# Output matmuls dealt over the last head, query rotations ahead of a normalisation, modulation sums in two halves: a two-block fp32 network on one Trainium2 core

## What is computed

```python
# first block (layers one and two): attention of the second branch, and the merge of three branches
q = rms_norm(q, qn_g); k = rms_norm(k, kn_g)
q, k = rope_2d(q, tabs), rope_2d(k, tabs)
s = jnp.einsum('bqkgd,bskd->bkgqs', q, k) * (ATT_HD ** -0.5)
p = jax.nn.softmax(s, axis=-1)
...
xs = xs + gate_x * ((sigmoid(p[13]) * ya + sigmoid(p[14]) * yb + sigmoid(p[15]) * yc) @ w_out)

# second block (layers three and four): four mLSTM heads, four retention heads, one output product
ada = c_act @ w_ada[l] + b_ada[l]
shift, scale, gate = jnp.split(ada, 3, axis=-1)
...
y = jnp.concatenate([y_m, y_r], axis=-1) @ w_out[l]       # (512, 2048) @ (2048, 1024)
x = x + gate * y
```

## Time and profile before

| what | us |
|---|---|
| median of three runs | 3299.59 (3297.2 to 3299.6) |
| the profiled execution, its own time | 3300.26 |
| its span | 3298.3 |
| PE busy | 3164.9 (96%) |
| DVE busy | 1366.0 (41%) |
| POOL busy | 1539.9 (47%) |
| ACT busy | 846.0 (26%) |
| mean granted TensorE clock | 0.978 |

### The profile page before, as it was taken

The page is one execution under the profiler, slowest core; times in us unless marked ns, Lnnn a source line. Parts: engine busy times, 40 slices in busy tenths (PEclk is TensorE's granted clock), DMA queues, the critical chain, the costliest instruction groups (busy, mean ns, idle before and its releaser), DMA issues.

```text
span 3298.3 us, 40515 instructions
## 1 busy us (share of the span) xinstructions
PE 3164.9 (96%) x15123; PEld 2302.9 (70%) x15123; DVE 1366.0 (41%) x2573; ACT 846.0 (26%) x1547; POOL 1539.9 (47%) x1451
## 2 busy tenths in 40 slices
PE   7999998999999999998989999999998999999989
PEld 4666675665656555465778768888994688889955
DVE  3021346544564412226666555444332363443322
ACT  4122226421111022324411222332111123322111
POOL 1688987000000059971353325776550157775600
PEclk9999999999999999998999999999999999999999
DMA  6111110023443121110233422222221222222202
GB/s 222 52 39 32 31 35 14 14 79 125 128 138 130 41 64 39 45 39 1 68 115 116 140 66 77 72 70 77 65 77 51 66 77 77 65 77 65 76 28 75
DMA packets 259907, 236.59 MB, mean 72 GB/s; under 512 B 20950, under 2 KB 257410, under 8 KB 259716
## 3 DMA queue, kind: packets, MB, share of 16 engines
q1 hardware_dynamic: 259716, 234.02, 23.4%
HBM read 231.91 MB, written 2.10 MB: 71 GB/s over the span
## 4 chain that ended last, share of the span: by engine, by line
PE 86%; DVE 8%; POOL 2%; ACT 2%; issue 1%; SPq 1%; DMA 0%; DVEq 0%; ACTq 0%; POOLq 0%
PE ps L481 27%; PE ps L1219 23%; PE ps L526 11%; PE ps L1053 5%; PE ps L512 3%; DVE arena L1905 2%; PE ps L1277 2%; PE ps L796 2%; DVE arena L1909 1%; PE ps L1321 1%; PE ps L809 1%; ACT arena L1375 1%; PE ps L1158 1%; DVE bQz L1909 1%; DVE small L2176 1%
## 5 line engine op out<-in xcount | busy, mean ns | idle before, releaser
L2604 POOL TENSOR_TENSOR arena<-arena,posi 128x512 f32<-128x512 f32 (+1 forms) x360 | 412.3, 1145 | 30.0
L481 PE MATMUL ps<-hT,wring 128*128 128x512 f32 (+1 forms) x1184 | 406.4, 503 | 0.7 <-ACT arena L1375 0.7
L526 PE MATMUL ps<-hT,wring 128*128 128x512 f32 (+1 forms) x1024 | 376.9, 523 | 0.4 <-ACT arena L1375 0.2
L481 PEld LDWEIGHTS ps<-hT,wring 128*128 128x128 f32 x1184 | 228.3, 194 | 170.1 <-issue 155.5
L1375 ACT ACTIVATE arena<-ps 128x256 f32<-128x256 f32 (+4 forms) x395 | 171.6, 434 | 642.4 <-PE ps L481 235.2
L2686 POOL TENSOR_TENSOR arena<-wring 128x512 f32<-128x512 f32 x72 | 91.8, 1275 | 491.8 <-PE ps L1219 297.2
L526 PEld LDWEIGHTS ps<-hT,wring 128*128 128x128 f32 x1024 | 194.1, 194 | 154.0 <-issue 145.1
L481 PE MATMUL ps<-arena,wring 128*128 128x512 f32 (+1 forms) x768 | 278.7, 523 | 3.0 <-issue 3.0
L2603 POOL TENSOR_SCALAR posi<-arena,cols 128x512 f32<-128x512 f32 (+1 forms) x360 | 245.7, 683 | 35.4
L1905 DVE TENSOR_TENSOR arena<-arena 128x768 f32<-128x768 f32 (+7 forms) x120 | 171.2, 1426 | 192.8 <-ACT arena L1375 188.9
L1375 ACT ACTIVATE arena<-ps,cols 128x512 f32<-128x512 f32 (+2 forms) x172 | 100.8, 586 | 545.8 <-PE ps L481 298.6
(11 more groups left out here) (271 smaller groups left out, 5068.1 us busy)
## 6 DMA issues: line engine op xcount, KB each, us to landing
wring<-in_w_in SPq DMA_DIRECT2D x126, 1024.0 KB, 5.4
wring<-in_w_mod SPq DMA_DIRECT2D x24, 1024.0 KB, 8.6
wring<-in_w_out SPq DMA_DIRECT2D x24, 1024.0 KB, 5.8
wring<-in_w_ada SPq DMA_DIRECT2D x21, 1024.0 KB, 5.2
wring<-in_w_conv_out SPq DMA_DIRECT2D x7, 512.0 KB, 6.1
wring<-in_w_gla_out SPq DMA_DIRECT2D x7, 512.0 KB, 6.1
wring<-in_w_attn_out SPq DMA_DIRECT2D x7, 512.0 KB, 5.5
arena<-in_w_ada SPq DMA_DIRECT2D x3, 1024.0 KB, 5.2
```

The source lines that it names most:

```text
L481: last = eng.matmul(o_(out), a, b_, start=(i == 0), stop=(i == len(parts) - 1))
L526: mm = eng.matmul(bank[b][:, 0:n], w[:, k, j * P:(j + 1) * P], hT[:, k, t0:t0 + n], start=(k == 0), stop=(k == KD - 1))
L2604: pool.link(eng.tensor_tensor(dst, dst, scratch, ALU.add))
```

## The change

Four things change.

1. **Output matmuls.** `OUT_SHARES` deals the same 42 products (three tiles of 14) over all nine items of the last head: 3, 5, 4, 5, 4, 6, 4, 7 and 4. The wait for head 6's result stands at product 12 of tile 0 rather than at product 0, and product 0 waits for head 5. `claim(4, 5)` behind the three tiles is gone.
2. **Queries.** In both layers of the first block the rotations of queries 2 and 3, and the reciprocal of the query scale, come ahead of `gla_scaled` on DVE; on PE `turned("q", 2)`, a gate job and `turned("q", 3)` come ahead of `gla_spread`.
3. **POOL** waits for `gla_scaled` of layer two before its `four_sums` of `hT`.
4. **Merge of layer two.** Each modulation group is a generator that stops after four of its eight products. The first four run after `combine`, the other four in the next step between `corner_sums` and `combine`. In the first round the groups (loads and ends too) move one step later.

```diff
+OUT_SHARES = [3, 5, 4, 5, 4, 6, 4, 7, 4]
+def mod_steps(l, a):
+    late = l == 1 and a == 0
+    return ([[]] if late else []) + MOD_LOADS[l], ([[]] if late else []) + MOD_ENDS[l]
...
-            a = [[("out", n, j)] for j in range(OUT_EARLY)]
+            ends = np.cumsum(OUT_SHARES).tolist()
+            a = [[("out", n, e - share, e)] for e, share in zip(ends, OUT_SHARES)]
...
-                next(between, None)
-                gla_spread(l, 1)
                 turned("q", 2)
                 next(between, None)
                 turned("q", 3)
+                next(between, None)
+                gla_spread(l, 1)
...
-                        j = x[0]
-                        if j == 0:
-                            rings[0] = LAST_HEAD
-                        claim(7 - j)
...
-                        eng.wait_ge(*at(("ys", l, 6)))
-                        for k in range(14):
+                        rings[0] = LAST_HEAD
+                        for j, k in (divmod(i, 14) for i in range(*x)):
+                            if k == 0:
+                                claim(7 - j)
+                                w_out.append(weights(wv(I["w_out_2"][l], j * P, P), 16, P))
+                                out_plan.append(len(plan) - 1)
+                            if j == 0 and k in (0, 12):
+                                eng.wait_ge(*at(("ys", l, 6 if k else 5)))
                             eng.matmul(bank[7 - j][:, 0:TX], w_out[j][:, k, :], ys[:, k, :], start=(k == 0), stop=False)
...
-                claim(4, 5)
                 rings[0] = {"A": [0, 1], "V": [2, 6, 3, 1]}
...
                     for k in range(1, KD):
+                        if k == KD // 2:
+                            yield
+                            dve.stage("modulation")
                         stt(sums, w[:, k, :], cT[:, col0 + 8 * c + k:col0 + 8 * c + k + 1], sums, M_, A_,
...
+                sums = []
                 for i in range(len(MERGE7) - 2):
                     a, step = divmod(i, 6)
                     corner_sums(i + 1)
+                    for part in sums:
+                        for _ in part:
+                            pass
+                    dve.stage("merge")
                     combine(i + 2)
...
-                    for i in MOD_LOADS[1][step]:
-                        modulate(*mod_groups(l, a)[i])
+                    sums = [modulation_parts(*mod_groups(l, a)[i]) for i in mod_steps(l, a)[0][step]]
+                    for part in sums:
+                        next(part)
...
-                gla_scaled(l, 1)
-                m.mark(("branch", l, 1), *m.at[("gla out done", l, 1)])
-                rotated("q", 2)
-                rotated("q", 3)
                 u0 = units(l)[0]
                 eng.wait_ge(*at(("free", ("qss", l))))
                 rcp(qscale[:, :, u0:6, :], qscale[:, :, u0:6, :], ("q inverse", l))
+                rotated("q", 2)
+                rotated("q", 3)
+                gla_scaled(l, 1)
+                m.mark(("branch", l, 1), *m.at[("gla out done", l, 1)])
...
             eng.wait_ge(*at(("full", ("ag", 1, 3, "x"))))
+            eng.wait_ge(*at(("gla out done", 1, 1)))
             four_sums(quarter, h_sums1, ("h sums1",))
```

More of the change, by code:

```diff
@@ L1113, in _ @@
                     for a in range(4):
+                        loads, ends = mod_steps(l, a)
                         for step in range(6):
                             products7(2 + 6 * a + step)
-                            for i in MOD_ENDS[1][step]:
+                            for i in ends[step]:
                                 mod_finish(*mod_groups(l, a)[i])
-                            for i in MOD_LOADS[1][step]:
+                            for i in loads[step]:
                                 mod_load(*mod_groups(l, a)[i])
@@ L1627, in merge7 @@
                     a, step = divmod(g - 2, 6)
-                    for i in MOD_ENDS[1][step]:
+                    for i in mod_steps(l, a)[1][step]:
                         mod = mod_groups(l, a)[i]
@@ L1976, in modulate, with modulation_parts @@
             def modulate(L, g):
+                for _ in modulation_parts(L, g):
+                    pass
+            def modulation_parts(L, g):
+                dve.stage("modulation")
                 done, depth = mods_done[L > 1], 2
@@ L2274, in merge7 @@
                         next(angles, None)
-                    dve.stage("modulation")
-                    for i in MOD_LOADS[1][step]:
-                        modulate(*mod_groups(l, a)[i])
+                    sums = [modulation_parts(*mod_groups(l, a)[i]) for i in mod_steps(l, a)[0][step]]
+                    for part in sums:
+                        next(part)
                     dve.stage("merge")
```

2 lines of the change are left out of this document (removed).

## The result

The changed kernel took 3261.99 us, median of 4 runs (3258.34 to 3264.76), against 3298.39 (3294.52 to 3299.60): a ratio of 0.9891, 95% interval 0.9874 to 0.9908, faster by 1.1%. Run again later beside other runs of the kernel before it took 3258.24 against 3300.55, 0.9866 (0.9844 to 0.9889). The forecast was 3250.5, with a range of 3241 to 3268. The profiled execution took 3261.85, with a span of 3260.2; before they were 3300.3 and 3298.3. So 38.1 of the span went, where 49.2 were forecast.

A forecast was written before the change was run, and what follows sets the result against it. PE, busy for 96% of the span, was taken to bound the kernel, leaving its waits and half clock to win. Savings of 27.0, 19.2 and 3, together 49.2, took 3300.3 to 3251.1, as median 3250.5; range 3241 to 3268.

The forecast's parts named there:

- Output matmuls: Last heads of layers three and four: dealing the products covers PE's waits, 27.0 saved, bounds 25 to 28.5.
- Merge: Merge of layer two: PE's waits for DVE fall from 17.9 to 5.2, 19.2 saved with clock, bounds 8 to 26.
- The step on the claim: Last heads: the 1.48 wait ahead of tile 3 was the claim of bank 5, and goes with it.
- the two waits of 0.34 and the 1.41 that I left in place: Last heads: two waits inside value items, forecast at 0.33 each, and layer four's starting wait for ACT, 1.41, stay.
- The sum of waits for `arena`: Merge of layer two: PE's ten waits for DVE, 17.9 in all, become 5.2.
- the last group of a round: Merge, where `mout` groups begin: PE's corner products start the chain; waits of 0.8, 0.8, 1.1 and 0.8 stay.
- the new wait between `mout` groups: Merge, first round: one second half falls between two `mout` groups, where ACT leaves no gap; a new wait of 1.0.
- The small waits in the `mgate` steps: Merge: waits of 2.00, 2.06 and 1.84 have 2.1 less ahead of the corner sum, so 0.1 each stays.
- The clock term: Merge: behind the 6.19 wait PE ran at clock 0.50; 6 of the 7.1 lost comes back.
- second halves meet POOL: Merge rival, chance 0.14: half of twelve second halves run beside POOL, each 3.5 longer; merge gives nothing, total 3270.
- Queries ahead: Start of attention, layer two: first maximum 7.0 earlier, 4 lost to POOL's adds; 3 saved, bounds 7 saved to 4 lost.
- the sum: Whole kernel: 27.0 from the last heads, 19.2 from the merge and 3 from the attention start, 49.2 saved.

## Why the prediction was right, and where it was not

**Output matmuls: right.** 27.0 forecast, 26.9 measured, with the distance at 51.90 and 52.01 against 51.7, the two waits of 0.34 and the 1.41 that I left in place. The step on the claim is confirmed by putting it back. Not all of it is waits, though. The distances of 66.1 and 63.6 held half clock, which I set against pieces at full clock without naming it: 12.8 with PE busy in the two last heads before, none now, worth 6.3. Less half clock the two heads gave 10.6 and 10.0.

**Merge: mechanism right, 19.2 forecast, 15.0 measured.** The sum of waits for `arena` and at the new place came to 9.7, not 5.2. The step that failed is the one on the last group of a round, "the halves give nothing back beyond what ran late: I take 0.8, 0.8, 1.1 and 0.8": it is 1.15 and three times 1.69, together 2.7 more. I counted four products in the chain at 0.52 and missed POOL's `last_weight_sum`, which lies there at each transition and adds 0.87. A like miss is in the new wait between `mout` groups, 2.24 for 1.0, where four products took 3.48: beside them stand `last_weight_sum` with 0.89 and the start of a weight sum of 1.27. The small waits in the `mgate` steps are 0.17, 0.32 and 0.32 in all, not three of 0.1. The clock term went the other way: forecast 6, while all half clock left the stretch, 14.2 of it with PE busy, worth 7.0; with the 8.2 of waits that is about the 15.0. The rival "second halves meet POOL" was half true: not at random phases but at every transition, at 0.9 instead of 3.5 each.

**Queries ahead: right in the trace, not to be told from nothing in the time.** Less half clock the stretch gave 2.9, where 3 was forecast, and PE's waits in it fell by as much. The first maximum came 8.6 earlier against the key norms (38.55 before, 29.99 after). Against the kernel with the outputs alone, whose order is that of before and whose half clock there is 13.7 as after, it is 6.9 (36.90), where 7.0 was forecast. The multiplies took 1.39 to 1.50. (The 0.69 of a simple add that the prediction names is the length of the one at 1521.57 of that timeline; the earlier trace rows do not show it.) The stretch itself gave 5.7; the 2.8 above the order's is half clock, which the forecast had left out. Alone the part gains nothing in ten runs.

**What the sum lacked.** 47.5 in the places of the change against 49.2 would have been a near hit, but in part by luck: 4.2 too little in the merge was set off by 2.7 too much at the queries, which is half clock. The sum then took it for granted that everything else stays, and this was the step that failed: 10.2 came back in unchanged stretches, nearly all of it half clock (54.7 there with PE busy for 35.0; 19.7 x 0.49 = 9.6). Where the change works, PE was busy at half clock for 32.6 less, worth 16.0, and 31.5 is waits and refills; in the whole span it was 13.6 less (109.9 for 123.5), worth 6.7. I booked recovered clock as a saving without asking whether the chip would lose it elsewhere. How much is lost differs from one execution to the next: the ten runs of the changed kernel took 3244.39 to 3264.76, so where in the range the measured time lies is partly chance.

## What to carry to other kernels

Work that fills another engine's gap should be cut to the gap in the trace (two products for 1.87 here), not in halves, and counted at its price beside whatever always runs at that phase. Recovered half clock is worth less than its place shows: compare kernels by the span less 0.49 of the half clock in which PE is busy, check that against the sum of PE's waits, and take the time itself from many runs. When a wait is removed, look at what the freed engine still does on every path (POOL's adds before, beside and behind the first maxima: 114.4, 114.0 and 112.8).

## What was not expected of the hardware

The granted clock falls in different executions behind different ones of the same PE events. The group stretches of layers three and four have three waits for ACT of 1.1 each, ahead of 128x128 products. In layer three of the changed kernel the clock fell behind the second and the third of them, and once at 2002.2, where there is no such wait. Behind the second, eight products took 3.16 (timeline of PE):

```profile
2151.14 0.71 PE L489 MATMUL ps<-arena 128*128 128x128 f32 x4 [1.09 <-ACT arena L1383]
2151.69 0.38 PE L1314 MATMUL ps<-const,arena 128*128 128x128 f32 x2
2151.91 3.16 PE L1228 MATMUL ps<-hT,wring 128*128 128x256 f32 x8
```

In the kernel with the queries alone the same wait, of the same length, was followed by full clock:

```profile
2160.91 0.71 PE L481 MATMUL ps<-arena 128*128 128x128 f32 x4 [1.08 <-ACT arena L1375]
2161.45 0.38 PE L1305 MATMUL ps<-const,arena 128*128 128x128 f32 x2
2161.67 1.89 PE L1219 MATMUL ps<-hT,wring 128*128 128x256 f32 x8
```

The same is seen in the windows (us; busy of PE, PEld, DVE, ACT, POOL; PEclk; DMA share; GB/s), of the changed kernel around that wait:

```profile
2144.00:2152.40 8.40, 7.31 (x35) 5.56 (x34) 2.88 (x7) 2.36 (x4) 6.09 (x7) 1.00 0.27 75
2152.40:2155.80 3.40, 3.40 (x10) 2.65 (x9) 0.29 (x1) 1.98 (x3) 3.32 (x2) 0.50 0.35 122
2155.80:2160.00 4.20, 4.20 (x21) 3.71 (x20) 0.42 (x1) 0.38 (x1) 3.82 (x4) 1.00 0.00 0
```

So the wait alone does not decide. That its moment does is a guess, and its rule stays open: no kernel was made to shift one stretch by a set amount. These waits for ACT, six of 1.1 and what half clock they bring, are the next thing that a change could remove; it was not tried.
